# A hybrid decoder step on one core: other division of the counted sets, a low key array of one copy, and query parts by GpSimd

## The reference

```
z = rmsnorm(x) @ w_in            # q, k, v, qi, ki, wi, ua, ub; partial rotary on q, k, qi, ki
score[t,s] = sum_h wi[t,h] * relu(qi[t,h] . ki[s] / 8), -inf where s is not visible
idx = the 256 best s of each t   # of the prompt's own keys, or of 2048 paged keys + 8
attn = softmax(q . k[idx] / 8) v[idx]     # 8 heads, 2 kv heads, head size 64
conv = swish(layernorm(depthwise31(ua * sigmoid(ub))))
x = x + rmsnorm(concat(attn, conv) @ w_out)
y = x + rmsnorm(relu(rmsnorm(x) @ w_up)^2 @ w_down)
```

## Time and profile before

| what | us |
|---|---|
| median of 3 runs (lowest, highest) | 1558.33 (1555.22, 1561.91) |
| the profiled execution's own time | 1556.52 |
| its span, first to last instruction | 1554.7 |
| busy in the span: PE | 1486.6 |
| busy: PEld, DVE, ACT, POOL | 1244.2, 688.2, 601.8, 453.0 |

### The profile page before, as it was taken

One profiled execution on the slowest core, in us unless ns is written; L12 is line 12 of the kernel. 1 busy time (PEld: TensorE's weight loads), 2 busy tenths in 40 slices (PEclk: granted clock), 3 DMA queues, 4 the chain that ended last, 5 costly groups with the idle time before them and its releaser, 6 DMA issues.

```text
span 1554.7 us, 22131 instructions
## 1 busy us (share of the span) xinstructions
PE 1486.6 (96%) x8490; PEld 1244.2 (80%) x8490; DVE 688.2 (44%) x1330; ACT 601.8 (39%) x1059; POOL 453.0 (29%) x458
## 2 busy tenths in 40 slices
PE   7998999999999998799999999999999999999995
PEld 4466446654878764588899999999999999999995
DVE  2429458788976564445532222222222222222234
ACT  3217548887567755554431211202212121120212
POOL 3233004442655325233312111211221121122124
PEclk9999999999999999999999999999999999999998
DMA  7021141432670017240011111111111111111112
GB/s 243 1 59 59 38 102 77 165 129 56 220 249 26 2 46 293 69 156 1 11 57 41 52 45 41 40 54 40 40 42 52 40 40 54 40 40 42 54 42 102
DMA packets 87812, 115.15 MB, mean 74 GB/s; under 512 B 11158, under 2 KB 72678, under 8 KB 84916
## 3 DMA queue, kind: packets, MB, share of 16 engines
q1 hardware_dynamic: 84252, 93.21, 18.7%
q0 software_dynamic: 3488, 20.98, 3.5%
HBM read 94.33 MB, written 20.16 MB: 74 GB/s over the span
## 4 chain that ended last, share of the span: by engine, by line
PE 55%; POOL 1%; DVE 1%; DMA 0%; issue 0%; ACT 0%; DVEq 0%; POOLq 0%; ACTq 0%
PE ps L2396 18%; PE ps L2398 18%; PE ps L2397 18%; PE ps L2431 0%; POOL y L2291 0%; DVE y L2566 0%; DMA out_y_p<-y 0%; POOL wlo L2255 0%; PE ps L2483 0%; DVE y L2576 0%; POOL stat L2266 0%; ACT whi L2305 0%; ACT hhi L2363 0%; POOL stat L2262 0%; DVEq L2565 0%
## 5 line engine op out<-in xcount | busy, mean ns | idle before, releaser
L2255 POOL TENSOR_TENSOR wlo<-wraw,whi 128x1024 fp32r<-128x1024 f32 x62 | 148.9, 2402 | 566.4 <-ACT whi L2305 566.4
L2397 PE MATMUL ps<-xlo,whi 128*128 128x384 f32 (+1 forms) x768 | 250.3, 326 | 0.0
L2396 PE MATMUL ps<-hhi,whi 128*128 128x384 f32 (+1 forms) x720 | 235.1, 327 | 0.8 <-POOL wlo L2255 0.8
L2398 PE MATMUL ps<-hhi,wlo 128*128 128x384 f32 (+1 forms) x720 | 235.2, 327 | 0.0
L2397 PE MATMUL ps<-hlo,whi 128*128 128x384 f32 (+1 forms) x720 | 234.9, 326 | 0.0
L2305 ACT CAST whi<-wraw 128x1024 fp32r<-128x1024 f32 x62 | 65.1, 1050 | 293.8 <-PE ps L2398 293.8
L2543 DVE TENSOR_TENSOR rel<-rel 128x384 f32<-128x384 f32 (+1 forms) x96 | 51.5, 537 | 283.7 <-ACT rel L2371 283.7
L2371 ACT ACTIVATE rel<-ps 128x384 f32<-128x384 f32 (+1 forms) x96 | 45.4, 474 | 264.3 <-PE ps L2398 264.3
L2397 PEld LDWEIGHTS ps<-xlo,whi 128*128 128x128 f32 x768 | 144.2, 188 | 0.0
L2396 PEld LDWEIGHTS ps<-hhi,whi 128*128 128x128 f32 x720 | 135.2, 188 | 1.1 <-POOL wlo L2255 1.1
L2398 PEld LDWEIGHTS ps<-hhi,wlo 128*128 128x128 f32 x720 | 135.1, 188 | 0.0
(11 more groups left out here) (315 smaller groups left out, 2792.0 us busy)
## 6 DMA issues: line engine op xcount, KB each, us to landing
wraw<-in_w_up SPq DMA_DIRECT2D x32, 512.0 KB, 4.0
wraw<-in_w_down SPq DMA_DIRECT2D x32, 512.0 KB, 3.4
taps<-qT SPq DMA_DIRECT2D x9, 960.0 KB, 4.0
hT<-taps SPq DMA_DIRECT2D x7, 960.0 KB, 4.7
x<-in_x SPq DMA_DIRECT2D x13, 512.0 KB, 7.4
w<-in_w_u SPq DMA_DIRECT2D x2, 2048.0 KB, 8.1
wo_raw<-in_w_out SPq DMA_DIRECT2D x8, 512.0 KB, 4.1
out_y_p<-y SPq DMA_DIRECT2D x8, 512.0 KB, 2.6
```

Of the source, the lines that this page charges most:

```text
L2255: nc.gpsimd.tensor_tensor(wlo_of(j, last), raw[:], whi_of(j, last), ALU.subtract).then_inc(s_wlo, 1)
L2396: nc.tensor.matmul(o, wh, xh, start=first, stop=False)
L2397: nc.tensor.matmul(o, wh, xl, start=False, stop=False)
L2398: return nc.tensor.matmul(o, wl, xh, start=False, stop=last)
```

## The change

It does five things:

- `ACT_SETS` is (0, 5, 6) for (2, 5, 6): ScalarE counts the set of 384 columns in place of the one of 640, VectorE the other way round. The constants `start` and `goal` follow from it.
- `SIDE_PACE` is 2.18 for 2.08: the units stand behind steps 1, 3, 5, 7, 9, 11, 14, 16, 18, 20, 22, 24 and the first queries behind 27, 28, 29.
- `kL` is one array of 128 partitions x 1,024 for both kv heads, without zeros. ScalarE copies the rounded keys into it, ahead of the copies for `kH`, and VectorE subtracts in place. GpSimd's two memsets go.
- The low product takes the 64 partitions of its kv head alone, of the queries and of `kL`.
- The low query parts of the second block are made by GpSimd at the start of the attention stage, ahead of the page loads, and no longer by VectorE in the selection stage. ScalarE still copies both blocks' high parts.

```diff
--- before.py
+++ after.py
@@ -87,8 +87,8 @@
 MK_OFF = [P * (i * (i + 1) // 2) for i in range(SEQ // P)]
 MK_COLS = P * (SEQ // P) * (SEQ // P + 1) // 2
 
-ACT_SETS = (2, 5, 6)
-SIDE_PACE = 2.08
+ACT_SETS = (0, 5, 6)
+SIDE_PACE = 2.18
 
 PH = 8
 CG = P // PH
@@ -163,8 +163,8 @@
 
                 w0 = sb_in(weights, "w0", [P, KC, 512])
             m["keys"] = sb_in(qkv, "keys", [P, 2 * NKV * SEQ], F32R)
-            m["kH"], m["kL"] = [m["keys"][:, i * NKV * SEQ:(i + 1) * NKV * SEQ].rearrange("p (k t) -> p k t", k=NKV)
-                                for i in range(2)]
+            m["kH"] = m["keys"][:, 0:NKV * SEQ].rearrange("p (k t) -> p k t", k=NKV)
+            m["kL"] = m["keys"][:, NKV * SEQ:(NKV + 1) * SEQ]
             with ExitStack() as normed:
                 m["hT"] = sb_in(normed, "hT", [P, KC, T])
 
@@ -967,9 +967,6 @@
                 diagonal(g, wdiag[g])
             for i in range(RT):
                 rotate(i)
-            pool.wait_ge(s_z, RT)
-            for kv in range(NKV):
-                nc.gpsimd.memset(kL[(1 - kv) * HD:(2 - kv) * HD, kv, :].bitcast(F32), 0.0)
 
         @block.scalar
         def _(act):
@@ -1056,6 +1053,7 @@
             for i in range(RT - 3, RT):
                 take_turn(i)
                 take_conv(i - RT + 3)
+            nc.scalar.copy(kL, kT[:, 0:SEQ]).then_inc(s_kh, 1)
             for kv in range(NKV):
                 for half in (kv, 1 - kv):
                     nc.scalar.copy(kH[half * HD:(half + 1) * HD, kv, :], kT[kv * HD:(kv + 1) * HD, 0:SEQ]).then_inc(s_kh, 1)
@@ -1266,17 +1264,14 @@
                     last = nc.vector.scalar_tensor_tensor(out=dst, in0=shaped(j, tie[q % 2], s, "n (p r) -> n r p"),
                                                           scalar=BIG, in1=dst, op0=ALU.mult, op1=ALU.add)
                 last.then_inc(s_tadd, 1)
+            dve.wait_ge(s_kh, 1)
+            nc.vector.tensor_tensor(kL, kT[:, 0:SEQ], kL, ALU.subtract)
+            i = SEQ // P - 1
             for kv in range(NKV):
-                rows = slice(kv * HD, (kv + 1) * HD)
-                dve.wait_ge(s_kh, 2 * kv + 1)
-                nc.vector.tensor_tensor(kL[rows, kv, :], kT[rows, 0:SEQ], kH[rows, kv, :], ALU.subtract)
-            for r in range(2):
-                i = SEQ // P - 1 - r
-                for kv in range(NKV):
-                    rows, low = slice(kv * HD, (kv + 1) * HD), slice((1 - kv) * HD, (2 - kv) * HD)
-                    dve.wait_ge(s_qh, NKV * r + kv + 1)
-                    nc.vector.tensor_tensor(qS[low, r, kv, :, :], qT[rows, :, i * P:(i + 1) * P],
-                                            qS[rows, r, kv, :, :], ALU.subtract).then_inc(s_ql, 1)
+                rows, low = slice(kv * HD, (kv + 1) * HD), slice((1 - kv) * HD, (2 - kv) * HD)
+                dve.wait_ge(s_qh, kv + 1)
+                nc.vector.tensor_tensor(qS[low, 0, kv, :, :], qT[rows, :, i * P:(i + 1) * P],
+                                        qS[rows, 0, kv, :, :], ALU.subtract).then_inc(s_ql, 1)
 
 
 def phase_attend(nc, st, sem, sb_in, ps, bank, m, a, out):
@@ -1472,9 +1467,10 @@
                 i = heads[r * NH][0]
                 if r >= 2:
                     pool.wait_ge(s_s, NH * (r - 1))
-                for kv in range(NKV):
-                    rows = slice(kv * HD, (kv + 1) * HD)
-                    nc.gpsimd.tensor_copy(qS[rows, r % 2, kv, :, :], qT[rows, :, i * P:(i + 1) * P]).then_inc(s_qh, 1)
+                    for kv in range(NKV):
+                        rows = slice(kv * HD, (kv + 1) * HD)
+                        nc.gpsimd.tensor_copy(qS[rows, r % 2, kv, :, :], qT[rows, :, i * P:(i + 1) * P]
+                                              ).then_inc(s_qh, 1)
                 for kv in range(NKV):
                     rows, low = slice(kv * HD, (kv + 1) * HD), slice((1 - kv) * HD, (2 - kv) * HD)
                     pool.wait_ge(s_qh, NKV * r + kv + 1)
@@ -1491,6 +1487,9 @@
 
             nc.gpsimd.memset(bq[:], 0.0).then_inc(s_z, 1)
             nc.gpsimd.tensor_copy(knew[:], kT[:, SEQ:T]).then_inc(s_z, 1)
+            pool.wait_ge(s_z, 2)
+            split_query(1)
+            pool.wait_ge(s_ql, NKV * 2)
             for b in range(2):
                 load(a["cache_k"], kpage[:, b, :], b, s_kp[b])
             for b in range(2):
@@ -1700,10 +1699,11 @@
                 if j >= 2:
                     pe.wait_ge(s_m, j - 1)
                 q = qS[:, j // NH % 2, kv, g, :]
+                rows = slice(kv * HD, (kv + 1) * HD)
                 for c, (s, n) in enumerate(key_chunks(P * (i + 1))):
                     o = bank[2 * (j % 2) + c][:, 0:n]
                     nc.tensor.matmul(o, q, kH[:, kv, s:s + n], start=True, stop=False)
-                    last = nc.tensor.matmul(o, q, kL[:, kv, s:s + n], start=False, stop=True)
+                    last = nc.tensor.matmul(o, q[rows, :], kL[rows, s:s + n], start=False, stop=True)
                 last.then_inc(s_s, 1)
 
             def turn(j):
```

## The result

The kernel after takes 1614.55 us (median of 6 runs, 1601.45 to 1617.90) beside 1558.09 us for the kernel before on the same chip: a ratio of 1.0349 (95% interval 1.0325 to 1.0373), 56 us slower. The forecast of 1587 (1566 to 1594) had the direction and half of the size.

What follows compares the result with a forecast made beforehand. TensorE was taken to bound the selection stage and attention loop, nearly. -1.7 us and +31.8 us gave +30.1 on the profiled execution's 1556.5 us, 1586.6; the forecast was 1587 us, range 1566 to 1594.

Steps and rivals of the forecast that it cites:

- The bound: Selection stage and attention loop: TensorE sets both ends, nearly, with 5.6 and 5.0 us unused.
- The counting, the tail and the queries: Selection stage and second block's query parts: -1.7 us for the stage, bounds -5.6 and +2; nothing for the query parts.
- the 1.67 us wait: Selection stage: TensorE's wait for ScalarE's two copies behind the counting goes, as the counting ends 4 us sooner.
- The 1.0 us off the rotation's wait: Selection stage: TensorE's 2.53 us wait for GpSimd's rotation gets 1.0 us shorter, bounds 0 and 2.5.
- The 1.0 us charged for ScalarE's copy: End of selection stage: the added 128x1024 copy delays the convolution's copy and SyncE's stores, +1.0 us.
- The later copies of the new pace: Selection stage: units 6 to 11 and three query copies come one step later; costed at nothing, some 2 us otherwise.
- -1.7: Selection stage's net change in us: -1.7 of TensorE's wait, -1.0 of the rotation's, +1.0 for ScalarE's copy.
- Query parts by GpSimd: Head of the attention stage: two subtractions hold the page loads back by 2.6 us; no cost forecast.
- The change of shape and the exposed load: Attention loop's score products: 192 changes and 128 exposed loads at 0.10 us each, 19.2 and 12.8 us.
- the transposes: Attention loop: 64 transposes behind a change of shape take 0.06 us more each, 3.8 us.
- the unused time: Attention loop: TensorE leaves 5.0 us unused, of which 4 is taken off the 35.8 us cost.
- a rival with a chance of 0.04: Attention loop: gaps lower TensorE's granted clock to 0.94, 8 us more, kernel at 1595 us; chance 0.04.

Runs made afterwards that it cites:

- the wide product: Changed kernel with the low key part as before: two arrays with zeros, low product over 128 channels; 1555.92 us, ratio 0.9977.
- the products by shape: Changed kernel with both high products of a head first, then both low ones; 1598.95 us, ratio 1.0241.
- the run on 64 rows throughout: Changed kernel with the high product also over the 64 partitions of its kv head; 1587.15 us, ratio 1.0186.
- the run with half the columns: Kernel before with the low product for the first 64 queries of each block alone, on all 128 rows; 1558.88 us, ratio 1.0008.
- the pairs: Changed kernel with two heads together: all high products, then low ones alternating between upper and lower 64 partitions; 1561.35 us, ratio 1.0025.
- the last version above: Kernel with everything but the narrow product, with heads paired from the fifth on in blocks 7 to 4; 1557.8 us, ratio 0.9997.
- the one line alone: Kernel before with one edit: the low product takes the 64 partitions of its own kv head; 1621.01 us, ratio 1.0398.
- the pairs on one half: Kernel with all heads in pairs, both low products of a pair on partitions 0 to 63; 1571.0 us, ratio 1.0084.
- the last four blocks: Kernel before with the 64-row low product only in blocks 3 to 0; 1578.16 us, ratio 1.0146.

## Where the prediction held and where it failed

- **The bound** was right: TensorE had 5.0 us to give in the loop, gave 3.7 (forecast 4), and what its products lost beyond that the kernel lost.
- **The counting, the tail and the queries**: the step got 0.21 us shorter (forecast 0.20), the 1.67 us wait went. The 1.0 us off the rotation's wait was wrong in sign (2.7 to 3.8 us). The 1.0 us charged for ScalarE's copy was not paid. The later copies of the new pace cost nothing, as forecast: no wait for them shows. So -1.7 became -0.3 in the profile; with the wide product these parts together gave a ratio of 0.9977, some 3.6 us, of which the counting alone and the query parts alone show nothing measurable (0.9991, 1.0002); where the rest of it is was not found. Query parts by GpSimd: nothing forecast, nothing measured.
- **The change of shape and the exposed load**, 0.10 us each: right. Forecast per head +0.70 and +0.30, measured +0.66 and +0.285; 35.8 us forecast with 3.8 for the transposes, 30.3 + 3.2 = 33.5 measured. With the unused time taken off, 31.8 was forecast and 29.8 measured. The run with the products by shape confirms the count, the run on 64 rows throughout shows that the price goes with the change. That the load price could be read from a change of columns held in size; but the run with half the columns shows that 64 of the lower columns alone do not bring it, so why the first score product stands 0.33 us before the second in the earlier trace rows is open. The value products ahead of it write the lower and the upper 64 partitions in turn, which that run did not.
- **The step that failed is the clock.** The sum was made at 2.4 GHz throughout. A lower clock in the loop was a rival with a chance of 0.04, priced at 8 us by a stretch at 0.94. It came: 70 of the loop's 192.9 us were at 1.2 GHz, and it cost some 24.9 us in the loop and 3.4 behind it, since the level is 0.5 and not 0.94: that figure was a mean over 30 us with 3.4 us at half. The row should have been opened for its levels before it was used as a price. The rival's reason, that the gaps between products lower the clock, is not shown.
- **A slip in the sum**: 1586.6 us is for an execution 1.8 us under the median, so the forecast should have read 1588; it does not matter here.
- The Trainium skill's rule cited in the prediction (TensorEngine Tiling (Array Packing), Key Properties: a change of mode drains) is borne out by the 0.43 us distances, for changes of rows. If a product of 64 columns counts as another mode, the columns' run speaks against it: 128 to 64 columns and back cost nothing there. The same section's statement that different tiles can work in parallel is seen in the pairs (0.61 us for four).

**What lowers the clock is narrowed down, not settled.** One execution of each kernel was traced, so what follows rests on one trace each; the mean clocks of the other executions, given above, vary.

*At the start of the loop* the fall itself, in after, can't be the work of the narrow product: the clock fell at 438.8 us, 0.4 us before the first score product. With wide products it falls near there in some kernels and for 3.4 us (at 440.9 us with the query parts alone, at 438.7 in the last version above, whose first heads are wide) and in the kernel before not at all. What goes with the narrow product is that it stays low: 23.9 us in after, 20.5 with the one line alone, 13.7 with the products by shape, 23.9 with all of them on 64 rows, 13.7 in the pairs on one half.

*Late in the loop* the narrow product brings the fall: the one line alone does, all the rest without it doesn't, and the last four blocks alone are enough. TensorE was not idle there (65.96 of 66.09 us busy around the fall in after, 37.67 of 37.80 before it in the last four blocks' kernel). Half-used columns don't bring it. Counted by changes of rows per head, into 64 or out of them, the runs fall in an order: four and two in after, two with the products by shape, two with all of them on 64 rows, two in the last four blocks; all of these have a late stretch of 27 us or more. Both kernels with all heads in pairs have one per head, and neither has it. That speaks for the changes and against rows that merely stand idle, which the pairs on one half have without a late stretch.

But those pairs have the 13.7 us at the start, where the pairs on both halves have none longer than 3.4, and between these two the count of changes is the same. So idle rows may count for something too. A change of rows without idle rows was not tried, and how the two add up stays open.

## What to carry to other kernels

Cutting a product from 128 to 64 channels saves no time on TensorE, and between full products each change of rows costs 0.10 us and exposes a load of 0.10. If the zeros are to go, put products of the two halves next to each other, where they overlap. And when an edit narrows products in a stage that TensorE fills, add a case in which part of the stage runs at 1.2 GHz: here that was about half of the loss, without TensorE going idle.

## What the runs showed of the hardware that I had not expected

- Products at 1.2 GHz in the alternation are 0.73 us apart for 0.43. Without a change of shape they are 0.43 apart there (all products on 64 rows) for 0.23, so the change and the load take 0.30 us at 1.2 GHz and 0.20 at 2.4.
- In after the clock is back at full from 462.7 to 585.6 us, in the middle of the same alternation, and falls again for blocks 1 and 0, where a head has 256 and 128 columns.
- The clock can be low for 51.2 us while TensorE's busy share stays at nine tenths or more.
- Going from 128 to the lower 64 columns and back is free; four 64-row products on two halves take 0.61 us instead of 1.01 on one.
